# The first layer's differential attention: the first softmax map is scaled on GpSimd instead of VectorE, and VectorE copies an output before it adds the second map

## The chip, the cores and the metric

The kernel runs on one core of a Trainium2 chip. The metric is the device time of one execution in microseconds (us). Before the change it is 2885.19 us, the median of three runs (2884.97 to 2889.27).

## What is computed

Two small transformer stacks of two layers each, on 256 latent tokens of width 1024 (the first stack has 256 context tokens beside them). The change lies in the mixer of the first layer of the first stack, a differential attention with 8 heads. Each head has two query-key maps of width 64 and one value of width 128:

```python
def diff_attend(q, k, v, lam):
    s = jnp.einsum('bqhmd,bkhmd->bhmqk', q, k).astype(jnp.float32) * ATTN_SCALE
    p = jax.nn.softmax(s, axis=-1)
    w = (p[:, :, 0] - lam * p[:, :, 1]).astype(v.dtype)
    return jnp.einsum('bhqk,bkhe->bqhe', w, v)
```

The latent queries see 512 keys, the context queries see 256. Everything is float32. Behind the attention each head's output is normalised (`rms_norm` with `subln_g`), and goes through the output projection. The other mixers (a neighbourhood attention in the second layer, and a forgetting, a sparse, a stick-breaking and a cross attention in the second stack) and the feed-forward blocks are not touched.

## The kernel before, in words

Each engine has its own instruction stream, written out by hand, and semaphores tie them together. Weights stream through a ring of three slots (`ring`), which SyncE fills; ScalarE and VectorE split each float32 block into a high and a low part (`Wh`, `Wl`, L1245 and L1685), and TensorE multiplies in three passes (L688). There is no planner: the order of the work is the order in which the loops issue it, and an engine that waits holds up all that stands behind it in its stream.

The attention of the first layer is a loop over 32 *units*, a head and a block of 128 queries. `units("diff")` gives four to a head, in the order 512, 512, 256, 256 keys. So units 4h and 4h+1 have 512 keys and units 4h+2 and 4h+3 have 256. In step i of its loop

- TensorE makes the two score maps of unit i (`Lb<-pv`, written by L653), transposes the weights of unit i-2 (L658, from `Pb`, after a wait for `pn_ready`), multiplies unit i-3 by the values (L653, output in `pv`), and then does what `head_sums` holds: the sum of squares of a head, and in five steps of eight a piece of the modulation (L800 and two small L653 products), which needs `w_mod` weights and serves later layers. `pa` and `pv` are two pools of four PSUM banks.
- VectorE takes the negated row maximum of both maps of unit i and copies them to `Lb` (L1823). Then it normalises unit i-1: the reciprocal of both row sums (L1829), the second one times -lambda (L1834), the first map times its reciprocal (L1835), the second map times its factor added to it (L1836, which sets `pn_ready`). Then it copies the output of unit i-3 from PSUM to `Oa` (L1667). In one step of four, i = 4h+10, `head_norms` adds the Newton step and scaling of head h (L1743, L1744, L1745, L1928), all 128x512; in another the low part of a head (L1692).
- ScalarE takes the exponentials of both maps of unit i with their row sums (L1331), does its part of the head norm (L1402, L1276, L1277, L1279, L1251) and of the modulation (L1308 into `BIG`, L1320), and moves the transposed weights of unit i-2 to `PT` (L1308).
- GpSimd has no part in this stage. In the second layer's attention (L2240) it scales the second map of each unit, 128x512, when `rr_ready` says that the reciprocal is there, while VectorE scales the first one (L1871). In its stream nothing but loads of small parameters comes before the first layer; then it waits for the end of the first layer's feed-forward block.

`Pb` holds six maps, three units of two, `rr` and `rs` three units. `step(...)` issues an instruction and makes VectorE wait for its end.

Of the kernel before, what the change touches and what calls it, by code (L numbers as in the profile page):

```python
# [25 lines left out]
ALU = mybir.AluOpType  # L26
# [170 lines left out]
def units(kind):  # L197

    if kind == "diff":
        return [(h, t, 512 if t >= 2 else 256) for h in range(DA_HEADS) for t in (2, 3, 0, 1)]  # L200
    if kind == "mem":
        return [(h, t, 256) for h in range(CA_HEADS) for t in range(2)]

    return [(h, t, P * (t + 1)) for h in range(N_FOX + N_DSA) for t in range(2)]
# [12 lines left out]
def stick_step(i, lag):  # L217


    h, rest = divmod(i - lag, 2)  # L220
    return h if rest == 0 and 0 <= h < N_SB else None
# [41 lines left out]
def program(nc, I, out):  # L263
    ctx = ExitStack()
    with ctx:
# [9 lines left out]
        def place(name, shape, dt=F32):  # L275
            t = over(name, shape, here[0], dt)
            here[0] += (4 * int(np.prod(shape[1:])) + 31) // 32 * 32
            assert here[0] <= start + ARENA, name
            return t
# [3 lines left out]
        def sem(name):  # L283
            sems[name] = ctx.enter_context(nc.semaphore(name))
            return sems[name]
# [29 lines left out]
        Pb = place("Pb", [P, 6, 512])  # L315
# [6 lines left out]
        rs = place("rs", [P, 3, 2])  # L322
        rr = place("rr", [P, 3, 2])
# [12 lines left out]
        def C(name):  # L336
            a, n = CONST[name]
            return con[:, a:a + n]
# [38 lines left out]
        def quarter(t, j):  # L377

            return t[:, j // 2, j % 2 * S:(j % 2 + 1) * S]
# [52 lines left out]
        qn_ready = sem("qn_ready")  # L432
        q_ready = sem("q_ready")
        rr_ready = sem("rr_ready")
        dv_ready = sem("dv_ready")
        p_ready = sem("p_ready")
        pn_ready = sem("pn_ready")
# [202 lines left out]
        def spread(x, dims):  # L640

            return bass.AP(tensor=x.tensor, offset=0, ap=[[0, P]] + dims)
# [1006 lines left out]
        def _(dve):  # L1649
            seen = Seen()  # L1650
            steps = [0]
            v = nc.vector

            def step(ins):

                steps[0] += 1
                ins.then_inc(dve_step, 1)
                dve.wait_ge(dve_step, steps[0])
# [4 lines left out]
            def copy_in(key, dst, src, lo=None):  # L1663

                dve.wait_ge(v_full, V.nth(key))
                b = V.bank(key)
                ins = v.tensor_copy(dst, src(b))  # L1667
                if lo is not None:
                    step(ins)
                    ins = v.tensor_tensor(lo, src(b), dst.bitcast(F32), ALU.subtract)  # L1670
                ins.then_inc(v_free, 1)
# [140 lines left out]
            def attention(tag, kind, todo, mask, scale, o_dst, also=lambda i: None):  # L1812


                maps = 2 if kind == "diff" else 1
                for i in range(len(todo) + 3):
                    if i < len(todo):
                        n = todo[i][2]
                        for m in range(maps):
                            key = (tag, "S", i, m)  # L1820
                            dve.wait_ge(v_full, V.nth(key))
                            b = V.bank(key)
                            v.tensor_tensor_reduce(Lb[:, i % 2 * 2 + m, 0:n], b[:, 0:n], mask(*todo[i]), -scale, -NEG,  # L1823
                                                   ALU.add, ALU.min, nm[:, i % 2, m:m + 1]).then_inc(v_free, 1)
                    if 0 <= i - 1 < len(todo):
                        u = i - 1
                        n = todo[u][2]
                        dve.wait_ge(p_ready, seen.more(p_ready, maps))
                        step(v.reciprocal(rr[:, u % 3, 0:maps], rs[:, u % 3, 0:maps]))  # L1829
                        p0 = Pb[:, u % 3 * 2, 0:n]  # L1830
                        if maps == 1:
                            v.tensor_scalar(p0, p0, rr[:, u % 3, 0:1], None, ALU.mult).then_inc(pn_ready, 1)
                        else:
                            step(v.tensor_tensor(rr[:, u % 3, 1:2], rr[:, u % 3, 1:2], lamt[:, 5:6], ALU.mult))  # L1834
                            step(v.tensor_scalar(p0, p0, rr[:, u % 3, 0:1], None, ALU.mult))  # L1835
                            v.scalar_tensor_tensor(p0, Pb[:, u % 3 * 2 + 1, 0:n], rr[:, u % 3, 1:2], p0,  # L1836
                                                   ALU.mult, ALU.add).then_inc(pn_ready, 1)
                    if i >= 3:
                        h, t, _ = todo[i - 3]
                        r, *dst = o_dst(h, t)  # L1840
                        copy_in((tag, "O", i - 3), dst[0], lambda b: b[r, 0:P], *dst[1:])
                    also(i)

            def sub(h):
# [211 lines left out]
            def mixer(l):  # L2056
# [92 lines left out]
                def mix_place(h, t):  # L2149
                    return two_heads(O_AT["fox"])(h, t) if h < N_FOX else two_heads(O_AT["dsa"])(h - N_FOX, t)  # L2150

                attention(("mix", l, "att"), "mix", units("mix"), mix_mask, 1.0, mix_place, beside)
                for i in range(len(units("mix")) + 3, MIX_STEPS):
                    beside(i)
# [60 lines left out]
        @block.gpsimd  # L2215
        def _(pool):
            def mask_columns(c, n):
                x = bias[c][:, n // 4, n % 4, :]
                nc.gpsimd.tensor_tensor(x, x, C("ncol"), ALU.add).then_inc(bias_ok, 1)

            nc.gpsimd.memset(cT, 0.0).then_inc(c_zero, 1)
            for tile, p0, n, lo, hi, src in row_loads:
                pool.dma_start(rowt[p0:p0 + n, tile, lo:hi], src).then_inc(rows_in, 16)
            for j, name in enumerate(("a_lambda_q1", "a_lambda_k1", "a_lambda_q2", "a_lambda_k2")):
                pool.dma_start(lamv[:, j, :], spread(I[name], [[1, HEAD]])).then_inc(small_in, 16)
            pool.dma_start(bfg[:, :, :], spread(I["b_fgate_2"], [[N_FOX, DEPTH], [1, N_FOX]])).then_inc(small_in, 16)


            pool.wait_ge(const_in, 16)
            pool.wait_ge(v_free, V.nth((("dn", 0, FF1 // P // CHUNK - 1), KT - 1)))  # L2230
            for c in range(2):
                for dst, src in bias_rows(c):
                    pool.dma_start(dst, src).then_inc(bias_in, 16)
                pool.wait_ge(bias_in, (c + 1) * 16 * 16)
                for n in range(8):
                    mask_columns(c, n)
            for s in range(len(NEAR_STEPS)):
                pool.wait_ge(rr_ready, s + 1)
                p = Pb[:, s % 3 * 2 + 1, :]
                nc.gpsimd.tensor_scalar(p, p, rr[:, s % 3, 1:2], None, ALU.mult).then_inc(pn_ready, 1)  # L2240
                if s in (0, 4):
                    pool.wait_ge(bias_late[s // 4], 16 * 16)
                if s < 8:
                    for n in range(s % 4 * 2, s % 4 * 2 + 2):
                        mask_columns(2 + s // 4, n)
            pool.wait_ge(v_free, V.nth((("att", 1), "O", len(NEAR_STEPS) - 1)))
            pool.dma_start(posi[:, :], spread(I["positions_2"], [[1, S]])).then_inc(pos_in, 16)
            pool.dma_start(memtok[:, :, :], I["mem_2"][0].rearrange("(t p) d -> p t d", p=P)).then_inc(mem_in, 16)

            for l in range(DEPTH):  # L2250
                for step_ in range(STICK_STEPS):
                    h = stick_step(step_, 3)
                    if h is not None:
                        z = Z[:, h % 3, :]
                        pool.wait_ge(z_dif, l * N_SB + h + 1)
                        nc.gpsimd.tensor_tensor(z, z, C("before"), ALU.mult).then_inc(z_one, 1)  # L2256
                    h = stick_step(step_, 6)
                    if h is not None:
                        w = TMP[:, h % 2, :]
                        pool.wait_ge(z_exp, l * N_SB + h + 1)  # L2260
                        nc.gpsimd.tensor_tensor(w, w, C("before"), ALU.mult).then_inc(z_att, 1)
                for n in range(KT):
                    pool.wait_ge(m_hi, l * KT + n + 1)
                    nc.gpsimd.tensor_tensor(quarter(HTl, M_AT[n]), TMP[:, n % 2, 0:S],
                                            quarter(HTh, M_AT[n]).bitcast(F32), ALU.subtract).then_inc(m_ready, 1)
# [52 lines left out]
```

## Time and profile before

| | |
|---|---|
| median of three runs | 2885.19 us |
| profiled execution, its own time | 2884.77 us |
| span of that execution in the profile | 2882.9 us |
| TensorE busy | 2700.4 us (94%) |
| VectorE busy | 1728.7 us (60%) |
| ScalarE busy | 1284.5 us (45%) |
| GpSimd busy | 128.6 us (4%) |

The busy share of an engine is an average over stages that have different limits. The chain of work that ended last is followed back from the last instruction to whatever released it, and so tells which engine set the time in each stretch. The attention loop that is changed runs from about 252 us to about 401 us of the span, some 5% of it.

### The profile page before, as it was taken

The numbers are of one execution on the slowest core, as the hardware profiler recorded it, in microseconds if no ns is written. First come the engines' busy times: TensorE is split into PE (matmuls) and PEld (weight loads), VectorE is DVE, ScalarE is ACT, GpSimd is POOL, SyncE is SP. The second block draws the span as 40 slices with busy tenths as digits, with TensorE's granted clock in tenths as the row PEclk, the third lists the DMA queues.
The fourth block names the chain that finished last, engine by engine and source line by source line (L and its number), as shares of the span: only waits on it lengthen the run. The fifth ranks groups of instructions, "written<-read, shape, count | busy, mean of one in ns | idle before, by whom it ended". The sixth has DMA issues, their size and how long they took to land.

```text
span 2882.9 us, 45579 instructions
## 1 busy us (share of the span) xinstructions
PE 2700.4 (94%) x18789; PEld 2406.9 (83%) x18789; DVE 1728.7 (60%) x3256; ACT 1284.5 (45%) x2348; POOL 128.6 (4%) x146
## 2 busy tenths in 40 slices
PE   5998889999989889999989989999999999899998
PEld 4776467888867679999989779899999997698998
DVE  4554765544566466676554766676565547666764
ACT  3544544232245454454443445554444434445543
POOL 1000000000040320000000011000000000110000
PEclk9999889999989899999999999999999999999999
DMA  7555432232252324556554314365665543144654
GB/s 243 191 175 161 146 116 74 89 102 97 93 103 88 88 76 161 166 171 183 168 158 143 111 58 147 118 172 167 189 186 165 171 138 115 58 142 126 167 167 121
DMA packets 511518, 397.09 MB, mean 138 GB/s; under 512 B 21848, under 2 KB 487008, under 8 KB 511184
## 3 DMA queue, kind: packets, MB, share of 16 engines
q1 hardware_dynamic: 508512, 387.10, 44.3%
q0 software_dynamic: 2080, 3.53, 0.9%
q8 instruction: 150, 2.46, 0.4%
q10 hardware_dynamic: 720, 3.54, 0.3%
q14 instruction: 56, 0.46, 0.0%
HBM read 393.08 MB, written 1.05 MB: 137 GB/s over the span
## 4 chain that ended last, share of the span: by engine, by line
PE 83%; DVE 9%; ACT 4%; issue 1%; POOL 1%; DMA 1%; SPq 0%; DVEq 0%; ACTq 0%
PE pv L688 42%; PE pa L688 30%; PE pv L653 5%; PE pa L653 3%; DVE Wl L1685 2%; ACT Wh L1245 1%; PE pa L800 1%; PE pa L658 1%; DMA ring<-in_w_mod_dram 1%; ACT Pb L1331 1%; DVE Lb L1823 1%; POOL BIG L2256 0%; POOL Pb L2240 0%; DVE TMP L1778 0%; DVE TMP L1756 0%
## 5 line engine op out<-in xcount | busy, mean ns | idle before, releaser
L1685 DVE TENSOR_TENSOR Wl<-ring,Wh 128x1024 fp32r<-128x1024 f32 (+3 forms) x688 | 767.6, 1157 | 350.5 <-ACT Wh L1245 348.3
L1245 ACT ACTIVATE Wh<-ring 128x1024 fp32r<-128x1024 f32 (+3 forms) x688 | 647.3, 990 | 507.7 <-PE pv L688 504.8
L688 PE MATMUL pa<-HTl,Wh 128*128 128x256 f32 (+1 forms) x1648 | 541.3, 328 | 43.9 <-DVE HTl L1763 26.7
L688 PE MATMUL pv<-HTl,Wh 128*128 128x256 f32 (+1 forms) x1872 | 547.1, 292 | 8.3 <-DVE XT L1803 2.3
L688 PE MATMUL pv<-HTh,Wl 128*128 128x256 f32 (+1 forms) x1872 | 538.3, 288 | 0.0
L688 PE MATMUL pv<-HTh,Wh 128*128 128x256 f32 (+1 forms) x1872 | 538.0, 287 | 0.0
L688 PE MATMUL pa<-HTh,Wl 128*128 128x256 f32 (+1 forms) x1648 | 525.1, 319 | 0.0
L688 PE MATMUL pa<-HTh,Wh 128*128 128x256 f32 (+1 forms) x1648 | 524.7, 318 | 0.0
L688 PEld LDWEIGHTS pa<-HTl,Wh 128*128 128x128 f32 x1648 | 325.6, 198 | 76.6 <-issue 40.9
L688 PEld LDWEIGHTS pv<-HTl,Wh 128*128 128x128 f32 x1872 | 360.4, 192 | 21.3 <-issue 7.5
L688 PEld LDWEIGHTS pv<-HTh,Wl 128*128 128x128 f32 x1872 | 360.7, 193 | 3.2 <-issue 0.5
L688 PEld LDWEIGHTS pv<-HTh,Wh 128*128 128x128 f32 x1872 | 360.6, 193 | 2.7
L688 PEld LDWEIGHTS pa<-HTh,Wl 128*128 128x128 f32 x1648 | 325.7, 198 | 20.1 <-issue 1.4
L688 PEld LDWEIGHTS pa<-HTh,Wh 128*128 128x128 f32 x1648 | 324.7, 197 | 18.5
L1308 ACT ACTIVATE BIG<-pa 128x256 f32<-128x256 f32 (+1 forms) x206 | 78.6, 387 | 311.5 <-PE pa L688 303.6
L688 PE MATMUL pv<-HID2l,Wh 128*128 128x256 f32 x704 | 199.2, 283 | 0.0
L688 PE MATMUL pv<-HID2h,Wl 128*128 128x256 f32 x704 | 199.2, 283 | 0.0
L688 PE MATMUL pv<-HID2h,Wh 128*128 128x256 f32 x704 | 199.2, 283 | 0.0
L688 PE MATMUL pv<-HID1l,Wh 128*128 128x512 f32 (+1 forms) x512 | 172.0, 336 | 0.0
L688 PE MATMUL pv<-HID1h,Wl 128*128 128x512 f32 (+1 forms) x512 | 172.0, 336 | 0.0
L688 PE MATMUL pv<-HID1h,Wh 128*128 128x512 f32 (+1 forms) x512 | 172.0, 336 | 0.0
L1793 DVE SCALAR_TENSOR_TENSOR XT<-pv,MOD,XT 128x256 f32<-128x256 f32 x216 | 95.7, 479 | 114.7 <-PE pv L688 113.9
(223 smaller groups left out, 4056.0 us busy)
## 6 DMA issues: line engine op xcount, KB each, us to landing
ring<-in_ffn_w_gu_dram SPq DMA_DIRECT2D x176, 512.0 KB, 5.1
ring<-in_w_mlp_dram SPq DMA_DIRECT2D x64, 1024.0 KB, 5.3
ring<-in_w_in_dram SPq DMA_DIRECT2D x54, 1024.0 KB, 5.2
ring<-in_w_mod_dram SPq DMA_DIRECT2D x48, 1024.0 KB, 5.7
ring<-in_ffn_w_down_dram SPq DMA_DIRECT2D x64, 704.0 KB, 4.6
ring<-in_a_w_qkv_dram SPq DMA_DIRECT2D x12, 1024.0 KB, 5.3
ring<-in_b_w_qkv_dram SPq DMA_DIRECT2D x12, 1024.0 KB, 5.2
ring<-in_w_out_dram SPq DMA_DIRECT2D x8, 1024.0 KB, 5.0
```

The lines of the kernel that those rows point to most:

```text
L653: m = nc.tensor.matmul(o, lhsT=lhsT, rhs=rhs, start=start, stop=stop)
L658: m = nc.tensor.transpose(o, x, C("ident"))
L688: m = nc.tensor.matmul(o, lhsT=x, rhs=y, start=first and j == 0, stop=last and j == 2)
L800: m = nc.tensor.matmul(b[32 * j:32 * j + 32, 0:256], lhsT=cT[:, k, :], rhs=w[:, k, :], start=k < 4, stop=k >= 4)
L1245: ins = nc.scalar.activation(Wh[rows, p % SPLIT, a:b], ring[rows, i % RING, a:b], ACT.Copy)
L1308: nc.scalar.activation(dst, src(b), func, scale=scale).then_inc(a_free, 1)
L1331: nc.scalar.activation(Pb[:, i % 3 * 2 + m, 0:n], Lb[:, i % 2 * 2 + m, 0:n], ACT.Exp, bias=nm[:, i % 2, m:m + 1], scale=-1.0, accum_out=rs ...
L1685: ins = v.tensor_tensor(Wl[rows, p % SPLIT, a:b], ring[rows, i % RING, a:b], Wh[rows, p % SPLIT, a:b].bitcast(F32), ALU.subtract)
L1793: m = v.scalar_tensor_tensor(XT[:, k, half], b[:, at:at + S], MOD[:, i, gate * KT + k, w:w + 1], XT[:, k, half], ALU.mult, ALU.add)
L1823: v.tensor_tensor_reduce(Lb[:, i % 2 * 2 + m, 0:n], b[:, 0:n], mask(*todo[i]), -scale, -NEG, ALU.add, ALU.min, nm[:, i % 2, m:m + 1]).then ...
```

## The change

Three things are done, all in the attention of the first layer (`maps == 2`).

1. The multiplication of a unit's first map by its reciprocal is taken from VectorE and given to GpSimd, which waits for the new semaphore `rd_ready` (the reciprocal is there) and signals `pm_ready`.
2. VectorE copies the output of unit i-3 right after the small product with -lambda.
3. Only then does VectorE wait for `pm_ready`, and adds the second map of unit i-1.

For the attentions with one map the order of instructions is as before.

```diff
@@ VectorE, attention, step i
                         dve.wait_ge(p_ready, seen.more(p_ready, maps))
-                        step(v.reciprocal(rr[:, u % 3, 0:maps], rs[:, u % 3, 0:maps]))
                         p0 = Pb[:, u % 3 * 2, 0:n]
                         if maps == 1:
+                            step(v.reciprocal(rr[:, u % 3, 0:maps], rs[:, u % 3, 0:maps]))
                             v.tensor_scalar(p0, p0, rr[:, u % 3, 0:1], None, ALU.mult).then_inc(pn_ready, 1)
                         else:
+                            v.reciprocal(rr[:, u % 3, 0:maps], rs[:, u % 3, 0:maps]).then_inc(rd_ready, 1)
+                            dve.wait_ge(rd_ready, seen.more(rd_ready))
                             step(v.tensor_tensor(rr[:, u % 3, 1:2], rr[:, u % 3, 1:2], lamt[:, 5:6], ALU.mult))
-                            step(v.tensor_scalar(p0, p0, rr[:, u % 3, 0:1], None, ALU.mult))
-                            v.scalar_tensor_tensor(p0, Pb[:, u % 3 * 2 + 1, 0:n], rr[:, u % 3, 1:2], p0,
-                                                   ALU.mult, ALU.add).then_inc(pn_ready, 1)
                     if i >= 3:
                         h, t, _ = todo[i - 3]
                         r, *dst = o_dst(h, t)
                         copy_in((tag, "O", i - 3), dst[0], lambda b: b[r, 0:P], *dst[1:])
+                    if maps == 2 and 0 <= i - 1 < len(todo):
+                        u = i - 1
+                        n = todo[u][2]
+                        p0 = Pb[:, u % 3 * 2, 0:n]
+                        dve.wait_ge(pm_ready, seen.more(pm_ready))
+                        v.scalar_tensor_tensor(p0, Pb[:, u % 3 * 2 + 1, 0:n], rr[:, u % 3, 1:2], p0,
+                                               ALU.mult, ALU.add).then_inc(pn_ready, 1)
                     also(i)
@@ GpSimd
             pool.wait_ge(const_in, 16)
+            for u, (_, _, n) in enumerate(units("diff")):
+                p = Pb[:, u % 3 * 2, 0:n]
+                pool.wait_ge(rd_ready, u + 1)
+                nc.gpsimd.tensor_scalar(p, p, rr[:, u % 3, 0:1], None, ALU.mult).then_inc(pm_ready, 1)
             pool.wait_ge(v_free, V.nth((("dn", 0, FF1 // P // CHUNK - 1), KT - 1)))
```

## Rows read from the trace of the kernel before

**Rows 1.** The page: busy time by engine; the chain that ended last, by engine.
```profile
PE 2700.4 (94%) x18789; PEld 2406.9 (83%) x18789; DVE 1728.7 (60%) x3256; ACT 1284.5 (45%) x2348; POOL 128.6 (4%) x146
PE 83%; DVE 9%; ACT 4%; issue 1%; POOL 1%; DMA 1%; SPq 0%; DVEq 0%; ACTq 0%
```

**Rows 2.** Windows: length, busy us (instructions) of PE, PEld, DVE, ACT, POOL; clock; DMA.
```profile
240.00:401.00 161.00, 131.69 (x939) 84.22 (x938) 107.24 (x326) 89.95 (x268) 0.00 (x0) 0.88 0.46 151
401.00:2883.00 2482.00, 2361.27 (x16515) 2167.73 (x16513) 1502.13 (x2727) 1094.09 (x1876) 116.52 (x118) 0.97 0.44 131
289.33:326.60 37.27, 30.69 (x209) 18.68 (x210) 26.57 (x83) 21.39 (x65) 0.00 (x0) 0.87 0.45 144
```

**Rows 3.** Waits of VectorE, 253 to 391 us: us in all, times, longest.
```profile
DVE Lb L1823 <- PE pv L653: 57.4, 19, 25.3
DVE Oa L1667 <- PE pv L653: 2.5, 4, 0.8
```

**Rows 4.** The chain that ended last, in order of time: start, us, what.
```profile
328.20 0.75 DVE Pb L1836
...
332.00 0.33 DVE Lb L1823
```

**Rows 5.** Timeline of VectorE: start, us, instruction [idle before it <- releaser].
```profile
290.03 0.16 DVE L1829 RECIPROCAL rr<-rs 128x2 f32<-128x2 f32 x1
...
290.94 0.75 DVE L1836 SCALAR_TENSOR_TENSOR Pb<-Pb,rr 128x512 f32<-128x512 f32 x1
...
291.81 0.68 DVE L1743 SCALAR_TENSOR_TENSOR T<-RQ 128x512 f32<-128x512 f32 x1
...
295.33 0.16 DVE L1829 RECIPROCAL rr<-rs 128x2 f32<-128x2 f32 x1
...
296.11 0.48 DVE L1836 SCALAR_TENSOR_TENSOR Pb<-Pb,rr 128x256 f32<-128x256 f32 x1
...
296.72 0.68 DVE L1823 CUSTOM_DVE_ANT_0 Lb<-pv,con 128x512 f32<-128x512 f32 x1
```

**Rows 6.** Timeline of the second layer's attention: who scales, and who waits.
```profile
986.84 1.56 POOL L2240 TENSOR_SCALAR Pb<-Pb,rr 128x512 f32<-128x512 f32 x1
...
1022.36 0.16 DVE L1869 RECIPROCAL rr<-rs 128x2 f32<-128x2 f32 x1
...
1022.55 0.49 DVE L1871 TENSOR_SCALAR Pb<-Pb,rr 128x512 f32<-128x512 f32 x1
1022.61 1.86 POOL L2240 TENSOR_SCALAR Pb<-Pb,rr 128x512 f32<-128x512 f32 x1 [1.49 <-DVE rr L1869]
...
1024.52 0.42 PEld L658 LDWEIGHTS pa<-con,Pb 128*128 128x128 f32 x4 [0.26 <-POOL Pb L2240]
```

**Rows 7.** GpSimd products of two widths: count, ns (min/median/max), first and last start, form.
```profile
L2219 POOL TENSOR_TENSOR HTf<-HTf,con x8: 719/722/735, 985.5 to 998.1; 128x256 f32<-128x256 f32 x8
L2261 POOL TENSOR_TENSOR TMP<-TMP,con x10: 1287/1319/2250, 1695.2 to 2526.4; 128x512 f32<-128x512 f32 x10
```

**Rows 8.** Timeline of the first units: TensorE and VectorE.
```profile
261.20 0.66 PE L658 MATMUL pa<-con,Pb 128*128 128x128 f32 x4 [1.23 <-DVE Pb L1836]
...
269.20 0.16 DVE L1829 RECIPROCAL rr<-rs 128x2 f32<-128x2 f32 x1
...
271.33 0.66 PE L658 MATMUL pa<-con,Pb 128*128 128x128 f32 x4
```

**Rows 9.** Timeline of VectorE where it waits for TensorE.
```profile
306.97 0.29 DVE L1667 COPY Oa<-pv 128x128 f32<-128x128 f32 x1 [0.63 <-PE pv L653]
...
343.97 0.29 DVE L1667 COPY Oa<-pv 128x128 f32<-128x128 f32 x1 [0.35 <-PE pv L653]
...
384.70 0.42 DVE L1823 CUSTOM_DVE_ANT_0 Lb<-pv,con 128x256 f32<-128x256 f32 x1 [0.83 <-PE pv L653]
```

**Rows 10.** Timeline of TensorE: the same sixteen products at either clock.
```profile
315.67 1.07 PE L800 MATMUL pa<-ring,BIG 128*32 128x256 f32 x16
...
322.54 1.93 PE L800 MATMUL pa<-ring,BIG 128*32 128x256 f32 x16 [3.39 <-ACT RQ L1279]
```

More of the change, by code:

```diff
@@ L434, in program @@
         rr_ready = sem("rr_ready")
+        rd_ready = sem("rd_ready")
+        pm_ready = sem("pm_ready")
         dv_ready = sem("dv_ready")
```

## The prediction

> **What bounds the kernel now.** First the page: TensorE is busy 94% of the span and holds 83% of the chain that ended last, VectorE 9% [rows 1]. That average says nothing about the 150 us that are changed, so the stretches come next. Behind 401 us TensorE is busy 2361 of 2482 us. In the attention it is busy 132 of 161 us at a mean granted clock of 0.88, and GpSimd does nothing at all [rows 2]. So inside the attention nobody is saturated; the time is set by a relay, and behind it by TensorE. Whatever the attention gets longer, the rest starts later by the same amount, because nothing behind it is slack that could take it up.
>
> Third, who waits for whom. VectorE waits 57.4 us for score maps, 25.3 of them before the first unit [rows 3], which looks like ample room. The chain in order of time says where there is none: once per head it runs through VectorE without a break, from the row maxima through the normalisation of a unit, the copy, the four 128x512 operations of the head norm, to the next row maxima [rows 4]. The reader is to see that the chain holds L1836 there, at 328.20. The head norm falls in step 4h+10, where the unit normalised is 4h+9, and that one has 512 keys. The loop repeats every 8 units; one period takes 37.3 us [rows 2], and holds two such passages.
>
> **The change on VectorE alone.** Measured from the start R of the reciprocal, a unit of 512 keys has its addition (L1836) at R + 0.91 and the instruction behind the copy at R + 1.78; with 256 keys these are R + 0.78 and R + 1.39 [rows 5]. The change removes the scaling from between, and puts a trip to GpSimd there. The reciprocal and its wait stay, as does the small product; the new semaphore on the reciprocal takes the place of the old one, at no cost.
>
> The trip: GpSimd starts 0.25 us after the start of the reciprocal (1022.36 to 1022.61), and whoever waits for it starts 0.05 behind its end (1024.47 to 1024.52) [rows 6]; I take 0.06 for VectorE. The duration of the scaling itself is the one disputed size. 128x512 took 1.86 us where it started beside VectorE's own scaling, and 1.56 where no such instruction ran [rows 6]. In the new kernel VectorE no longer has a scaling at that moment, only a 128x1 product and a copy out of PSUM, so I take the value nearer to the free one, 1.60, and keep 1.56 and 1.86 as ends.
>
> For 128x256 there is no row of this operation. Products of two tensors took 0.72 us at 256 and from 1.29 us at 512 [rows 7], a proportion of 0.56, which gives 0.90 from 1.60. The ends: 0.72, the same width in that other operation, and 1.29, the 512 row. I take 0.90, since the rows of one operation at two widths are the nearest to what is asked.
>
> The Trainium skill speaks to this in "SBUF — State Buffer", section "SBUF: two separate sides": VectorE and GpSimd share one pair of ports, which is locked for a whole instruction when VectorE runs in a two-port mode. The trace agrees as far as it goes: the two durations above differ by 0.30 us, and the longer one is that which began inside VectorE's scaling of 0.49. With the lock in force as in the second layer the sum below would be that with 1.86.
>
> So with 512 keys the addition comes at R + 0.25 + 1.60 + 0.06 = R + 1.91, 1.00 us later than before. The copy (0.20) is done under the trip. Whatever follows comes 0.67 us behind the start of the addition (0.91 + 0.67 + 0.20 was R + 1.78), at R + 2.58: 0.80 later. With 256 keys the addition is at R + 1.21, 0.43 later, and the next instruction 0.41 behind it, at R + 1.62, 0.23 later. Where an output is not there yet, the copy now also holds up the addition, which in the old order went ahead; VectorE waited for an output 4 times, 2.5 us in all [rows 3], mostly in the last units.
>
> **Carried through one period**, from 289.33. In step 10 the head norm starts 0.80 late, and so do the next row maxima, which were back to back with it. Step 11 has 256 keys: a further 0.23 on VectorE, hidden behind ScalarE, which is busy until then. Steps 12 and 13 wait for TensorE, 0.80 late by now. Step 13 normalises 512 keys and step 14 again, with row maxima between and no wait: its addition is followed 3 x 0.80 = 2.40 us later than in the old order without waits. But in the old order the copy of step 14 waited 0.63 us for its output [rows 9], and as a record ends 0.08 behind the point where the next instruction starts (290.94 + 0.75 against 291.81 - 0.20 [rows 5]), there are 0.71 us of room: the head norm is 1.7 late, with it the row maxima of step 15, and through ScalarE's copy into PT also TensorE. Per period 1.7 us.
>
> The other stretches. Units 0 to 9: TensorE already waited 1.23 us for L1836 at 261.20 [rows 8], so there 1.00 counts in full. The unit normalised in step 5 has its reciprocal at 269.20 and is transposed at 271.33 [rows 8]; now the reciprocal is at 269.20 + 1.00 + 0.23, the addition 1.91 later, 0.75 long, and 0.06 to TensorE: 273.15, 1.8 late. Units 18 to 25: the wait is 0.35 [rows 9], 2.40 - 0.43 = 2.0, of which a short wait in front of the next row maxima takes up to 0.2 (an estimate): 1.8. Units 26 to 31: 2.4 less the 0.83 + 0.08 that VectorE had to spare at 384.70 [rows 9]: 1.5. Sum: 1.8 + 1.7 + 1.8 + 1.5 = 6.8 us. The same walk with 1.86 and 1.17 (0.90 and the lock's 0.30 rounded down) gives 2.6 + 2.5 + 2.6 + 2.2 = 9.9; with 1.56 and 0.72 it gives 1.6 + 1.6 + 1.7 + 1.4 = 6.3. 1.29 with 256 keys would add 0.4 to the first stretch and little to the others, where ScalarE covers that unit.
>
> What a reader would expect as a gain, 32 scalings taken from VectorE (16 with 512 keys at 0.49 us [rows 6], 16 shorter ones), is worth nothing, because each is replaced by a longer wait in the same stream. The copy that moves forward frees a bank of `pv` earlier, but TensorE never waited long for one.
>
> **The clock.** The waits of TensorE get longer, and its clock is already at half in places: sixteen products took 1.93 us at 322.54, behind 3.39 us idle, and 1.07 at 315.67 [rows 10]. Some added stretches at 1.2 GHz instead of 2.4 are likely. At 0.86 us per such group I allow one, 0.9 us; the ends are none and nine groups' worth, 8 us.
>
> Sum: 6.8 + 0.9 = 7.7 us on the profiled execution's own 2884.8 us, which is 0.4 below the median shown: 2892.5.
>
> **The rivals.**
>
> *Not slower: VectorE's waits swallow it.* The turning point is the duration d of the scaling with 512 keys: below 0.80 (0.25 + d + 0.06 + 0.67 = 1.78) no passage gets longer. If GpSimd did 128x512 in 0.6, the addition would come when it does now and each of seven passages would save the copy's 0.20: 2884.8 - 1.4 = 2883.4. Against it: 16 scalings of just this kind, none under 1.56 [rows 6]. The Trainium skill's "GPSIMD Engine Reference", section "Engine selection", calls a one-input operation on GpSimd roughly line-rate, which would be this case; the trace does not agree, with 1.56 us against VectorE's 0.49 [rows 6]. The chance is 0.04.
>
> *Partly swallowed.* My walk takes the passages as unbroken. If TensorE or ScalarE is what ends the waits in half of them (for it: the waits at 306.97, 343.97 and 384.70 [rows 9], and the 57.4 us of [rows 3]), half of 6.8 is left: 2884.8 + 3.4 = 2888.2. Chance 0.24.
>
> *The port is still contended*, by the small product or the copy: as it is in the second layer [rows 6]: 9.9 + 0.9, 2895.6. Chance 0.14.
>
> *The clock falls further*: the longer waits put more of the stage at half clock [rows 10], 6.8 + 8, 2899.6. Against it: the mean of 0.88 [rows 2] has held up with waits of 3 us in it. Chance 0.08.
>
> *GpSimd is not ready* or sits behind its loads: it had nothing to do between 240 and 401 us [rows 2]; no chance worth a number.
>
> **How the numbers follow.** The forecast has 0.50. About 0.2%, 5.8 us, is what a measurement of this kernel can tell from no change. Slower by more: the forecast's case nearly whole, the contended port and the clock, 0.72. Within: the partly swallowed case, the other side and a slice of the forecast, 0.25. Faster: 0.03. The range leaves out the other side and the bottom of the partly swallowed case below, and the clock above: 2887.5 to 2898.5.
>
> **What would show it.** In the changed profile: GpSimd has 32 scalings of 1.56 to 1.65 us (16) and about 0.9 (16) between 255 and 392 us. L1836 starts 1.9 us behind its reciprocal with 512 keys, 1.2 with 256, and VectorE's wait for GpSimd in front of it sums to 25 to 35 us. The period of 37.3 us becomes about 39, and the chain holds GpSimd's scaling in it, once or twice. Behind the attention nothing changes but the start. Wrong would be: a period of 37.3 to 37.8 (the waits swallowed it), scalings of 1.85, or a mean clock in the stage well under 0.85.

## The result and the profile after

The changed kernel takes 2898.81 us, median of five runs (2898.55 to 2900.24). Five runs of the kernel before, taken with them, have a median of 2889.27 (2884.97 to 2896.31); the ratio is 1.0040, with a 95% interval of 1.0025 to 1.0055. So the change costs 7 to 16 us: 9.5 by the two medians, 11.6 by the ratio. The profiled execution took 2900.01 us, span 2897.9; that of the kernel before took 2884.77, so these two are 15.2 apart, more than the medians.

Page of the kernel after, busy time by engine and the chain by engine (they answer to [rows 1]):
```profile
PE 2712.2 (94%) x18789; PEld 2412.0 (83%) x18789; DVE 1716.3 (59%) x3224; ACT 1285.7 (44%) x2348; POOL 169.1 (6%) x178
PE 82%; DVE 9%; ACT 4%; POOL 2%; issue 1%; DMA 1%; SPq 0%; DVEq 0%; ACTq 0%
```
VectorE has 12 us less work, as intended. TensorE has the same 18789 matmuls and is busy 11.8 us longer, which no line of the change asks for.

Windows of the attention, first row maxima to the first product of the output projection, of the kernel before and then of the kernel after, with everything from 410 us on in the last row (columns as in [rows 2]):
```profile
252.35:400.15 147.80, 118.49 (x832) 73.02 (x833) 106.42 (x325) 87.62 (x261) 0.00 (x0) 0.87 0.48 156
```
```profile
253.10:415.74 162.64, 130.23 (x833) 78.94 (x833) 94.41 (x293) 88.31 (x261) 39.83 (x32) 0.81 0.44 142
410.00:2883.00 2473.00, 2359.82 (x16504) 2165.51 (x16504) 1503.79 (x2724) 1093.74 (x1874) 117.12 (x118) 0.97 0.44 132
```
The stage is 14.8 us longer between these two executions. Behind it 2482.8 us are left of the span before and 2482.2 after, so nothing has changed there. TensorE is busy 11.7 us longer in the stage over the same matmuls, at a granted clock of 0.81 in place of 0.87, and idle 3.1 us longer.

VectorE's timeline after, a unit of 512 keys and one of 256 (it answers to [rows 5]); then GpSimd's scalings:
```profile
294.35 0.16 DVE L1836 RECIPROCAL rr<-rs 128x2 f32<-128x2 f32 x1
...
295.63 0.29 DVE L1669 COPY Oa<-pv 128x128 f32<-128x128 f32 x1 [0.93 <-PE pv L655]
296.20 0.75 DVE L1848 SCALAR_TENSOR_TENSOR Pb<-Pb,rr 128x512 f32<-128x512 f32 x1 [0.28 <-POOL Pb L2241]
296.87 0.68 DVE L1745 SCALAR_TENSOR_TENSOR T<-RQ 128x512 f32<-128x512 f32 x1
...
300.40 0.16 DVE L1836 RECIPROCAL rr<-rs 128x2 f32<-128x2 f32 x1
...
301.61 0.48 DVE L1848 SCALAR_TENSOR_TENSOR Pb<-Pb,rr 128x256 f32<-128x256 f32 x1 [0.53 <-POOL Pb L2241]
```
```profile
294.60 1.57 POOL L2241 TENSOR_SCALAR Pb<-Pb,rr 128x512 f32<-128x512 f32 x1 [6.03 <-DVE rr L1836]
300.65 0.92 POOL L2241 TENSOR_SCALAR Pb<-Pb,rr 128x256 f32<-128x256 f32 x1 [4.48 <-DVE rr L1836]
```
VectorE's waits in the kernel after, then TensorE's for the addition, before and after (waiter, releaser: sum in us, number, longest):
```profile
DVE Pb L1848 <- POOL Pb L2241: 19.8, 25, 1.7
DVE Oa L1669 <- PE pv L655: 15.1, 16, 2.0
```
```profile
PE pa L658 <- DVE Pb L1836: 2.5, 5, 1.2
PE pa L660 <- DVE Pb L1848: 7.1, 10, 1.3
```
The addition comes 1.85 us behind its reciprocal with 512 keys and 1.21 with 256 (14 of 16 and 10 of 16 units; the others, where the output was late, come up to 2.04 and 2.57 behind it). GpSimd takes 1.57 and 0.92.

The chain that ended last, of the kernel after, the passage of one head (start, us, what). The passage at 328.20 of [rows 4] had VectorE alone:
```profile
309.16 1.57 POOL Pb L2241
310.76 0.75 DVE Pb L1848
311.51 0.33 DVE Lb L1825
311.86 0.34 DVE Lb L1825
312.37 1.58 POOL Pb L2241
313.97 0.75 DVE Pb L1848
314.72 0.61 DVE T L1745
```
And TensorE's timeline, first two groups of the kernel before, then the same groups and others of the kernel after (it answers to [rows 10]):
```profile
313.72 1.16 PE L653 MATMUL pv<-PT,BIG 128*128 128x128 f32 x8 [0.89 <-ACT PT L1308]
314.71 1.02 PE L653 MATMUL pa<-SQ,con 128*128 128x512 f32 x2
```
```profile
302.83 1.86 PE L655 MATMUL pv<-PT,BIG 128*128 128x128 f32 x8 [0.25 <-ACT PT L1310]
304.48 1.91 PE L655 MATMUL pa<-SQ,con 128*128 128x512 f32 x2
...
319.92 0.48 PE L660 MATMUL pa<-con,Pb 128*128 128x128 f32 x2 [0.84 <-DVE Pb L1848]
321.18 2.07 PE L655 MATMUL pv<-PT,BIG 128*128 128x128 f32 x8 [0.78 <-ACT PT L1310]
323.04 1.91 PE L655 MATMUL pa<-SQ,con 128*128 128x512 f32 x2
324.89 1.94 PE L802 MATMUL pa<-ring,BIG 128*32 128x256 f32 x16
...
332.73 1.07 PE L802 MATMUL pa<-ring,BIG 128*32 128x256 f32 x16 [3.39 <-ACT RQ L1281]
```
The sixteen products of the modulation take 1.94 us at 324.89, as at 322.54 before, but this is the place of 315.67, where they took 1.07 [rows 10]. The two groups in front of them are at about half speed too (2.07 and 1.91 us in place of 1.16 and 1.02), behind waits of 0.84 and 0.78 us. The place of 322.54 is 332.73 here, and behind the same wait of 3.39 us the products now take 1.07. So the stretches at half speed have moved as well as grown, and the length of the last wait alone does not tell where they fall.

### The profile page after: what moved, and what is told of

The parts are those of the page before. It is cut to its first block, busy times and chain, and to the rows that moved or that the text cites. A ratio compares the mean times of both kernels' runs of the same rounds, so it can differ in the third digit from the quotient of the medians.

```text
span 2897.9 us, 45611 instructions
## 1 busy us (share of the span) xinstructions
PE 2712.2 (94%) x18789; PEld 2412.0 (83%) x18789; DVE 1716.3 (59%) x3224; ACT 1285.7 (44%) x2348; POOL 169.1 (6%) x178
## 4 chain that ended last, share of the span: by engine, by line
PE 82%; DVE 9%; ACT 4%; POOL 2%; issue 1%; DMA 1%; SPq 0%; DVEq 0%; ACTq 0%
PE pv L690 41%; PE pa L690 30%; PE pv L655 5%; PE pa L655 3%; DVE Wl L1687 2%; ACT Wh L1247 1%; PE pa L802 1%; PE pa L660 1%; DVE Lb L1825 1%; DMA ring<-in_w_mod_dram 1%; POOL Pb L2241 1%; POOL BIG L2268 0%; DVE HTl L1765 0%; ACT Pb L1333 0%; POOL Pb L2252 0%
## 5 line engine op out<-in xcount | busy, mean ns | idle before, releaser
L690 PEld LDWEIGHTS pa<-HTl,Wh 128*128 128x128 f32 x1648 | 325.1, 197 | 78.8 <-issue 42.3
```

The lines of the kernel that those rows point to most:

```text
L690: m = nc.tensor.matmul(o, lhsT=x, rhs=y, start=first and j == 0, stop=last and j == 2)
```

## The experiments

Three theories were open after this result. C: the trip to GpSimd delays seven passages of VectorE, and the waits that this gives TensorE put it at half clock, which costs again. Against it, G: GpSimd itself costs; and O: the copy, now in front, holds up the addition. The table sets side by side what each kernel's profile and runs gave. *Stage* is from the first row maxima to the first product of the output projection; *period* is the distance of the row maxima of units 10, 18 and 26, worked out from VectorE's timeline.

| kernel | median us (runs) | ratio to before, 95% | stage us | clock there | periods |
|---|---|---|---|---|---|
| before | see each set | | 147.8 | 0.87 | 37.3, 37.1 |
| after | 2898.81 (5) | 1.0040 (1.0025 to 1.0055) | 162.6 | 0.81 | 42.2, 41.5 |
| order_only | 2886.53 (12) | 0.9999 (0.9989 to 1.0009) | 150.2 | 0.90 | 37.6, 37.6 |
| pool_copy_last | 2902.49 (6) | 1.0049 (1.0033 to 1.0066) | 164.5 | 0.80 | 40.7, 41.5 |
| vec_delay | 2899.79 (8) | 1.0033 (1.0017 to 1.0048) | 167.1 | 0.79 | 42.3, 39.7 |
| vec_half | 2893.65 (12) | 1.0016 (1.0004 to 1.0028) | 157.3 | 0.84 | 39.5, 38.9 |
| fill_before | 2882.63 (11) | 0.9980 (0.9971 to 0.9990) | 144.9 | 0.94 | 34.8, 34.8 |
| fill_after | 2892.23 (11) | 1.0011 (1.0001 to 1.0021) | 155.2 | 0.89 | 38.2, 37.4 |
| ratio | 2886.06 (11) | 1.0002 (0.9991 to 1.0012) | 147.5 | 0.87 | 36.8, 37.8 |
| ratio_fill | 2881.04 (8) | 0.9976 (0.9966 to 0.9986) | 141.1 | 0.97 | 34.2, 34.2 |
| fill_before2 | 2883.01 (11) | 0.9980 (0.9970 to 0.9990) | 141.9 | 0.96 | 34.8, 34.8 |
| fill_after2 | 2892.59 (12) | 1.0015 (1.0005 to 1.0026) | 152.1 | 0.96 | 37.0, 38.0 |
| ratio_fill2 | 2878.26 (6) | 0.9964 (0.9950 to 0.9978) | 139.6 | 0.96 | 34.2, 34.2 |

The first set has four kernels with 25 runs of the kernel before (median 2888.82).

**order_only.**
```diff
                             step(v.tensor_scalar(p0, p0, rr[:, u % 3, 0:1], None, ALU.mult))
-                            v.scalar_tensor_tensor(p0, ..., ALU.mult, ALU.add).then_inc(pn_ready, 1)
                     if i >= 3:
                         ...
                         copy_in((tag, "O", i - 3), dst[0], lambda b: b[r, 0:P], *dst[1:])
+                    if maps == 2 and 0 <= i - 1 < len(todo):
+                        v.scalar_tensor_tensor(p0, ..., ALU.mult, ALU.add).then_inc(pn_ready, 1)
```


> One part of the change alone: VectorE keeps the scaling of the first map; only the copy of the output moves in front of the addition. No GpSimd. Theory C (the trip delays seven passages by 0.8 us each, about 6.5 us, and the longer waits of TensorE put it at half clock, some 6 to 8 us more): the addition comes 0.2 us later and what follows it at the same time as before, so the time stays within 2 us of the kernel before. Rival O (the copy in front holds up the addition when its output is late: in the changed kernel VectorE waited 16 times, 15.1 us, for an output, before 4 times, 2.5 us): 4 to 6 us slower than before. Rival G (GpSimd itself costs, by its port or its signals): within 1 us.


Measured: no difference; O's 4 to 6 us lie outside the interval. VectorE waits 11.8 us for outputs there, where it waited 3.6 in the same stretch of the kernel before, and the time does not show it. Probably what it waits for would have held it up a moment later anyway; that is argued, not shown. O falls.

**pool_copy_last.**
```diff
+                    (GpSimd scales, VectorE waits for pm_ready and adds, as in the change)
                     if i >= 3:
                         ...
                         copy_in((tag, "O", i - 3), dst[0], lambda b: b[r, 0:P], *dst[1:])
-                    (the addition behind the copy)
```


> The change with one part undone: GpSimd scales the first map, but the copy stays behind the addition as in the kernel before. Theory C: the copy's 0.20 us is no longer under the trip, seven passages, so 1.4 us slower than the changed kernel if the clock stays as it is there: 11 to 17 us slower than the kernel before. Rival O: the addition is no longer held up, 3 to 5 us faster than the changed kernel, some 5 to 8 above the kernel before.


Measured: 13.7 us over the kernel before by the medians. It is 3.7 us above the changed kernel by the medians, of different sets; the 1.4 us that C expected between them are not resolved. O, which asked for a kernel some 4 us faster than the changed one, fails a second time.

**vec_delay.**
```diff
                             step(v.tensor_scalar(p0, p0, rr[:, u % 3, 0:1], None, ALU.mult))
+                            for k in ((240, 120) if n == 512 else (48,)):
+                                step(v.tensor_tensor(pad[:, 0:k], C("ones")[:, 0:k], C("ones")[:, 0:k], ALU.mult))
                     (copy, then the addition, as in order_only)
```


> The delay without GpSimd: VectorE scales the first map itself and then works on small products of constants that nobody needs (128x240 and 128x120 with 512 keys, 128x48 with 256), until the addition comes as late behind the reciprocal as in the changed kernel (1.85 us with 512 keys, 1.2 with 256), with the copy in the same place. Theory C: as slow as the changed kernel, 11 to 15 us over the kernel before, with a mean clock of about 0.84 in the attention. Rival G: without GpSimd and its port the loss is the delay alone or less, at most 8 us.


Measured: 11.0 us over the kernel before by the medians, beside the change's 9.5. GpSimd is idle in this kernel's attention, and the loss is there all the same:
```profile
254.29:421.41 167.12, 134.10 (x832) 82.12 (x833) 120.19 (x373) 88.40 (x261) 0.00 (x0) 0.79 0.43 138
```
C had expected a clock of about 0.84; it is 0.79. The interval, 5 to 14 us, still holds G's 8, so the timed runs alone do not decide. The traces do, for one period: measured from the row maxima of unit 10, later ones come later than in the kernel before by (us, worked out from VectorE's timelines)

| row maxima of unit | 11 | 13 | 14 | 15 | 17 | 18 |
|---|---|---|---|---|---|---|
| after | 0.74 | 2.37 | 3.11 | 3.14 | 5.88 | 4.94 |
| vec_delay | 0.75 | 2.42 | 3.18 | 3.22 | 5.86 | 4.99 |
| fill_after2, against fill_before2 (both below) | 0.75 | 0.74 | 1.48 | 2.23 | 2.23 | 2.22 |

With GpSimd or without it the kernel is late by the same amounts to within 0.1 us. G falls: it is the time between reciprocal and addition that costs, whoever spends it.

**vec_half.**
```diff
-                            for k in ((240, 120) if n == 512 else (48,)):
+                            for k in ((180,) if n == 512 else (1,)):
```


> Half of that delay: one useless product 128x180 with 512 keys (0.38 us) and one 128x1 with 256 keys. If the loss is the delay alone, 7 passages by 0.38 give 2.7 us. Theory C: 2.7 us and a part of the clock's loss that need not be in proportion, 3 to 9 us. Rival O: as the order is the changed one, 4 to 6 us plus 2.7.


Measured: 4.8 us over by the medians, at a clock between the two. It is less than half of what the whole delay costs, and more than the 2.7 of the delay alone, but the interval (1.2 to 8.1 us) holds both.

The second set has 30 runs of the kernel before (median 2888.57). Its kernels give TensorE something to do where it would wait.

**fill_before** and **fill_after.** The edit is the same in the kernel before and in the changed one:
```diff
+            def filler(count, n=256):
+                if V.taken():
+                    pe.wait_ge(v_free, V.taken())
+                for _ in range(count):
+                    mm(V.banks[V.n % BANKS][:, 0:n], C("ones")[:, 0:P], C("ones")[:, 0:n], True, True)
...
+                        if kind == "diff" and i >= 8 and i % 8 == 6:
+                            filler(2)
                         pe.wait_ge(pn_ready, seen.more(pn_ready))
...
+                        if kind == "diff" and i >= 8 and i % 4 == 0:
+                            filler(1)
                         pe.wait_ge(a_free, A.nth((tag, "T", u)))
...
+                            if step_ % 8 == 1 and step_ > 8:
+                                filler(6)
                             next_modulation(n)
```


> The kernel before, and TensorE works while it would wait: from unit 8 on, products of constants (128x256, about 0.5 us each) into the PSUM bank that it takes next, six before the modulation in steps 9, 17, 25 (3.3 us idle there), two before the transposes in steps 14, 22, 30 (1.2 us idle), one before the values in every fourth step (0.7 us idle). They compute nothing that is used. Theory C: the granted clock of the attention rises from 0.88 towards 1, the half-speed groups (1.93 us for sixteen products in place of 1.07) disappear: 3 to 8 us faster than the kernel before. Against it: the clock does not depend on these waits, or the added products take more than they give: 0 to 5 us slower.

> The changed kernel with the same useless products in the same places. Theory C: what is left between it and the kernel before with these products is the delay alone, 6 to 8 us, in place of the 11 to 15 between the two kernels without them; so 0 to 4 us over the kernel before. If the rest of the loss is not the clock's, the distance between the two stays at 11 to 15 us.


Measured: the kernel before gets 5.9 us faster by doing 31 useless products (62 instructions of TensorE in the trace). Its period goes from 37.3 to 34.8. The changed kernel gets 6.6 us faster (2898.81 to 2892.23, in different sets), but the distance between the two stays at 9.6 us, where C expected 6 to 8. In its trace TensorE still waited 12.8 us for the addition and its clock was at 0.89: the products stand at the waits of the kernel before, and not at the new ones.

**ratio** and **ratio_fill.** The first map is not scaled at all. Each output is larger by its row sum, which the head norm takes out except for its epsilon; this part of the computation is changed.
```diff
-                        step(v.reciprocal(rr[:, u % 3, 0:maps], rs[:, u % 3, 0:maps]))
+                            step(v.reciprocal(rr[:, u % 3, 1:2], rs[:, u % 3, 1:2]))
...
-                            step(v.tensor_tensor(rr[:, u % 3, 1:2], rr[:, u % 3, 1:2], lamt[:, 5:6], ALU.mult))
-                            step(v.tensor_scalar(p0, p0, rr[:, u % 3, 0:1], None, ALU.mult))
+                            step(v.scalar_tensor_tensor(rr[:, u % 3, 1:2], rr[:, u % 3, 1:2], lamt[:, 5:6],
+                                                        rs[:, u % 3, 0:1], ALU.mult, ALU.mult))
```


> No engine scales the first map: the second one is added with -lambda times the quotient of the two row sums, so each output comes out larger by the first row sum, which the head norm behind it divides out but for its epsilon. VectorE loses the scaling (0.52 us from start to start with 512 keys, 0.39 with 256) and nothing is put in its place. Theory C: seven passages by 0.5 us, 3.5 us, and by the same rule in the other direction shorter waits and somewhat more clock: 3 to 8 us faster than the kernel before. If VectorE's passages did not set the time: no difference.

> The same without any scaling of the first map, and TensorE's useless products in its waits. Theory C: the two gains add up, 6 to 14 us faster than the kernel before. If the products now come where TensorE no longer waits: no better than the one without them.


Measured: without the useless products no difference (1.0002), against an expectation of 3 to 8 us faster. A lengthened passage of VectorE costs, a shortened one gave nothing that can be measured. The chain of this kernel shows part of the reason: in every second passage it does not come through the addition but through the copy of an output that TensorE made late, and so it did in the kernel before, at 306.97 [rows 9]:
```profile
342.54 0.46 PE pv L653 x4
343.02 0.29 DVE Oa L1667
343.31 0.61 DVE T L1743
```
The other part is the clock: the first period is 0.5 us shorter than before, the second 0.6 longer, with groups at half speed where they had been at full speed (2.07 and 1.80 us at 349.76 and 351.63, where the kernel before had 1.16 and 1.02). With the products the period falls from 34.8 to 34.2, so at the full clock there is a small gain. ratio_fill is 7.5 us faster than the kernel before, inside the 6 to 14 expected, but the two kernels with products (2882.63 and 2881.04) are not apart beyond their intervals, so the gain is that of the products.

The third set has 23 runs of the kernel before (median 2889.54).

**fill_before2** repeats fill_before for this set. **fill_after2:**
```diff
-                        if kind == "diff" and i >= 8 and i % 8 == 6:
-                            filler(2)
+                        if kind == "diff" and i >= 8 and i % 8 in (0, 3, 6):
+                            filler({0: 1, 3: 3, 6: 2}[i % 8])
```


> The kernel before with the useless products once more, to stand beside the next one on the same chip. In its trace the period of 8 units was 34.8 us with TensorE at full clock from 300 to 384 us, in place of 37.3. Every theory: 5 to 7 us faster than the kernel before, period 34.8.

> The changed kernel with more of the useless products, since in the first try TensorE still waited 12.8 us for the addition and fell to half clock there: in steps 3 of 8 three of them before the transposes, in steps 0 of 8 one more. Theory C: the clock of the attention is at 1 nearly throughout, and the period is that of the filled kernel before plus the delay alone, 34.8 + 1.6 to 2.2 = 36.4 to 37.0; the whole is 6 to 8 us over the filled kernel before, so 0 to 2 us over the unfilled one. If something else than the clock makes the second half of the loss, the period stays at 37.8 or more and the distance at 10 us.


Measured: fill_before2 is 6.5 us faster than the kernel before with a period of 34.8, as expected. Windows of the attention, of fill_before2 and then of fill_after2:
```profile
252.36:394.30 141.94, 121.46 (x894) 76.50 (x894) 105.87 (x325) 87.63 (x261) 0.00 (x0) 0.96 0.50 163
```
```profile
251.08:403.22 152.14, 129.96 (x921) 82.76 (x921) 94.30 (x293) 88.17 (x261) 39.75 (x32) 0.96 0.47 152
```
The clock of the stage is 0.96 in both. The first period, at full clock in both, is 37.0 beside 34.8, 2.2 us for the delay alone, where the two unfilled kernels are 4.9 apart (42.2 and 37.3). The second, 38.0, is 3.3 over, with a stretch at half clock in it. Up to the row maxima of the last unit the filled kernels are 9.4 us apart (135.9 and 126.5 from the first ones), the unfilled ones 14.8 (147.2 and 132.4). The medians of the timed runs are 9.6 apart again, at the same mean clock of 0.9688, and fill_after2 is 3.1 over the kernel before, not 0 to 2. So the periods are partly what C asked for, and the whole is not.

The table under vec_delay tells why 6 to 8 was too little. C took the delay alone for 6.8 us, and in that the copy of step 14 gave 0.71 us of room back. In the kernel before it waits 0.63 us for its output [rows 9]; in fill_before2 it does not wait:
```profile
306.28 0.28 DVE L1680 COPY Oa<-pv 128x128 f32<-128x128 f32 x1
```
So all three units of 512 keys in a period count there, 3 x 0.74 = 2.22. The products take away not only the half speed, but also a wait that had hidden a part of the delay. The last edit gave nothing measurable over fill_after; its four added products per period are partly work that TensorE must do outside its waits.

**ratio_fill2**, for a kernel that beats both:
```diff
@@ ScalarE, step 33
-                            if n == LATER_MOD:
-                                for _ in range(SPLIT):
-                                    prepare()
+                    (the same behind the copy into PT of that step)
@@ VectorE
-                        if modulation_step(step_ - 1) == LATER_MOD:
+                        if modulation_step(step_ - 2) == LATER_MOD:      # ahead of the head norm of step 34
                             for _ in range(SPLIT):
                                 prepare()
```


> A kernel that should beat both: no scaling of the first map (the outputs are larger by its row sum, which the head norm divides out but for its epsilon), TensorE's useless products in its waits, and at the end of the attention ScalarE moves the last transposed weights, and VectorE copies the last output, before they split the two weight blocks of the output projection (3.9 us on ScalarE, 4.6 on VectorE stood in front). 1 to 4 us faster than the same kernel without that last edit, which was 6 to 9 us faster than the kernel before. Against it: the weight blocks are then late for the projection, and it is no faster than that one.


Measured: 2878.26 us, 11.3 us faster than the kernel before in the same set (0.9964, interval 0.9950 to 0.9978), and faster than the changed kernel by about 20. The last edit's own share, 2.8 us by medians of two sets, is not separated from chance.

## Why the prediction was wrong

The direction was right, and most of the mechanism. The time, 2892.5 with a range to 2898.5, was too low: 2898.81. Of the 6.3 us, 4.4 are the base from which the sum started, and 1.9 the loss itself, 9.6 us over the median of all runs of the kernel before, where the sum had 7.7. Two terms failed: the base, and the 0.9 us allowed for the clock.

**The trip and its price on VectorE: right.** Forecast were 1.60 and 0.90 us of scaling, the addition 1.91 and 1.21 us behind the reciprocal; measured 1.57 and 0.92, 1.85 and 1.21. GpSimd started 0.25 us behind the reciprocal's start. The rival with a contended port (1.86) has no case: all 16 scalings of 512 keys took at most 1.57. Here the rule of the Trainium skill, "SBUF — State Buffer", "SBUF: two separate sides", agrees with the trace in the direction that the sum used: without a scaling of VectorE beside it GpSimd was not held.

**The walk: right for these kernels.** In the table under vec_delay the row maxima come 0.74 later behind the head norm of step 10 (forecast 0.80), again 0.74 later in step 13, and 0.03 in step 14, where the old order had its 0.71 of room: 1.5 us, where the sum had 1.7. In the next period these are 0.75, 0.74 and 0.14, or 1.6 for 1.8. The unit of 256 keys in step 11 adds nothing, as foreseen: in the filled pair unit 13 is no later than unit 11. One reading of [rows 4] was wrong: of the two passages in a period the chain of the kernel before runs through the addition only in one; in the other it comes from TensorE through the copy at 306.97. The sum had that wait in its 0.71, but the text counted two passages without a break. In the changed kernel the chain holds three scalings of GpSimd in this period (294.60, 309.16, 312.37), not one or two. VectorE's wait for GpSimd was forecast at 25 to 35 us and is 19.8, because a part of the time is spent waiting for outputs, 15.1 us.

**The clock: 0.9 us allowed, too little.** This term failed. It allowed one group at half speed. Between the profiled executions the rest of the first period, 4.94 - 1.51 = 3.4 us, is groups at half speed: those at 302.83 and 304.48 took 1.6 us more than before and those from 321.18 to 324.89 2.7 more, and the one at 332.73 took 0.9 less. In the second period the rest is 2.7. Over the whole stage it is 14.8 - 6.8, 8 us, and the sign of being wrong that the prediction named, a clock well under 0.85, came true with 0.81. That pair overstates it, since the kernel before was caught in one of its quicker executions. The runs tell it better, as each has its mean granted clock. In 78 runs of the kernel before, 2878.2 to 2895.8 us, time and clock go together with a correlation of -0.90, 1.9 us for each 0.001. Over all kernels the slope within a kernel is 1.8. The changed kernel had 0.9620 in the mean and the kernel before 0.9637: 3 us of the 10.7 between their means (2899.3 and 2888.6), which leaves 7.7 for the delay. This split is a fit over runs, not an experiment, and the mean clock of a span also counts stretches in which TensorE is idle. The filled pair, 9.6 us apart at one clock, cannot confirm it, since its delay is a larger one. So how much of the 10 us is the clock's in the timed runs, 3 or more, stays open.

**The base: 4 us too low.** The sum started from the profiled execution, 2884.8 us, and said that it was 0.4 under the median shown. Both lie in the lower part of the spread: the median of the 78 runs is 2889.2. Three runs, two of them within 0.3 us of each other, did not show that. This was more than the error of the loss: from 2889.2 the same sum gives 2896.9, inside the range. 2889.2 + 6.8 + 3 would have been 2899.

So of the rivals "the clock falls further" came nearest, with its mechanism real. Its size of 8 us fits the profiled pair and is too much for the runs, and that its 2899.6 lies so near is luck: 14.8 us of loss on a base 4.4 too low. "Partly swallowed" had no part in it beyond the room that the walk had counted; the delays of 0.74 arrive in full.

## What to carry to other kernels

Giving work of a busy engine to an idle one is worth nothing when the first must wait for the result in the same stream: what counts is the time from the cause to the signal, and here it went from 0.91 to 1.85 us. Look for the passage in which the chain stays on one engine, and price the edit there, not by busy time. A change that fills one engine's waits can also take away a wait that hid another delay, so two such edits need not add up. Where TensorE waits in a relay, its clock belongs to the sum with both signs, and the spread of a dozen runs with their clocks should be known before a profiled execution is taken as the base.

## What was not expected of the hardware

- Useless matmuls in TensorE's waits made the kernel before faster: 0.9980 twice (0.9971 to 0.9990 and 0.9970 to 0.9990), with the granted clock of the attention at 0.94 and 0.96 in place of 0.87. The group of sixteen products behind the longest wait took 1.07 us in place of 1.93, once the wait was down from 3.39 us to 0.80:
```profile
321.83 1.07 PE L800 MATMUL pa<-ring,BIG 128*32 128x256 f32 x16 [0.80 <-ACT RQ L1292]
```
The wait's length alone does not decide it: in the changed kernel, at 332.73, the same products took 1.07 us behind 3.39 as well.

- Thirty runs of one kernel on one chip spread over 17 us (2878.2 to 2895.0), most of it with the granted clock (a correlation of -0.92 in them).
- A 128x256 scaling on GpSimd takes 0.92 us beside 1.57 for 128x512, which makes 2.5 ns for each further element of a partition and 0.27 us before the first (worked out from these two widths).
